# A decoder step on one core: sample tokens' attention scores moved to TensorE, weight splits moved to VectorE, one value stripe moved behind the second turn

## The reference, cut to what matters

```python
def mem_kv(mem, g, w_kv):                       # 256 memory tokens, once
    kv = rmsnorm(mem, g) @ w_kv                 # 1024 x 2048 weights
    k, v = jnp.split(kv, 2, axis=-1)
    return (k.reshape(B, M, X_HEADS, X_HEAD_DIM), v.reshape(B, M, X_HEADS, X_HEAD_DIM))

def cross_attend(h, mk, mv, w_q, w_o):          # 4 heads of 256, M = 256
    q = (h @ w_q).reshape(B, L, X_HEADS, X_HEAD_DIM)
    s = jnp.einsum('blhd,bmhd->bhlm', q, mk) * (X_HEAD_DIM ** -0.5)
    p = jax.nn.softmax(s, axis=-1)
    o = jnp.einsum('bhlm,bmhd->blhd', p, mv)
    return o.reshape(B, L, D_MODEL) @ w_o
```

## Time and profile before

| | us |
|---|---|
| median of 3 runs (1449.26 to 1451.04) | 1449.39 |
| the profiled execution | 1445.97 |
| its span, first to last instruction | 1444.1 |
| PE busy in the span | 1409.5 |
| PEld (weight loads) busy | 1368.8 |
| DVE busy | 893.8 |
| POOL busy | 631.0 |
| ACT busy | 421.6 |

### The profile page before, as it was taken

How to read it: one execution, slowest core, us unless ns; L and a number is a source line. 1 busy time by engine, 2 the same in 40 slices (tenths; PEclk the granted TensorE clock), 3 DMA queues, 4 the chain that set the end, 5 groups by cost and what they waited for, 6 DMA issues and landing times.

```text
span 1444.1 us, 25449 instructions
## 1 busy us (share of the span) xinstructions
PE 1409.5 (98%) x9871; PEld 1368.8 (95%) x9871; DVE 893.8 (62%) x1465; ACT 421.6 (29%) x635; POOL 631.0 (44%) x479
## 2 busy tenths in 40 slices
PE   8999999999999996999999999999999999999997
PEld 7999999989999975889999999999999999999996
DVE  4325677778752268647997666766676658632335
ACT  6131344470020144520042222222223223311111
POOL 1241246045531166314572877787778710000163
PEclk9999999999999999999999999999999999999999
DMA  9412111102161266321123222122222142423113
GB/s 293 125 44 81 51 30 38 37 23 59 44 190 45 87 241 197 117 88 44 44 59 88 89 84 77 59 87 87 73 68 77 59 133 95 168 89 110 36 44 117
DMA packets 163567, 129.18 MB, mean 89 GB/s; under 512 B 11532, under 2 KB 148748, under 8 KB 163363
## 3 DMA queue, kind: packets, MB, share of 16 engines
q1 hardware_dynamic: 163499, 128.25, 28.6%
HBM read 107.88 MB, written 20.58 MB: 89 GB/s over the span
## 4 chain that ended last, share of the span: by engine, by line
PE 71%; POOL 10%; issue 9%; DVE 5%; ACT 2%; DMA 2%; SPq 1%; POOLq 0%; DVEq 0%; ACTq 0%
PE pm L2294 18%; PE pm L2296 18%; PE pm L2295 18%; PE pm L2565 3%; PE pm L2567 3%; PE pm L2566 3%; POOL gb L1040 2%; POOL raw L1022 2%; POOL raw_c L1022 2%; POOL sum L1029 1%; POOL sum L1027 1%; DMA xt<-in_x_prompt 1%; DVE acc L2210 1%; PE pm L2427 1%; POOL raw_c L1034 1%
## 5 line engine op out<-in xcount | busy, mean ns | idle before, releaser
L2294 PE MATMUL pm<-x_hi,w_hi 128*128 128x344 f32 x960 | 310.6, 323 | 0.3 <-DVE gb L1654 0.3
L2296 PE MATMUL pm<-x_hi,w_lo 128*128 128x344 f32 x960 | 306.6, 319 | 0.0
L2295 PE MATMUL pm<-x_lo,w_hi 128*128 128x344 f32 x960 | 306.6, 319 | 0.0
L1126 ACT ACTIVATE w_hi<-raw 128x1024 fp32r<-128x1024 f32 x88 | 93.3, 1060 | 531.7 <-PE pm L2296 455.1
L2294 PEld LDWEIGHTS pm<-x_hi,w_hi 128*128 128x128 f32 x960 | 180.4, 188 | 2.1 <-issue 1.5
L2295 PEld LDWEIGHTS pm<-x_lo,w_hi 128*128 128x128 f32 x960 | 180.4, 188 | 0.2
L2296 PEld LDWEIGHTS pm<-x_hi,w_lo 128*128 128x128 f32 x960 | 180.4, 188 | 0.0
L843 POOL TENSOR_TENSOR raw<-raw,gains 128x1024 f32<-128x1024 f32 x32 | 63.6, 1992 | 128.2 <-DMA raw<-in_w_in 81.3
L1587 DVE TENSOR_TENSOR w_lo<-raw,w_hi 128x1024 fp32r<-128x1024 f32 x79 | 112.9, 1429 | 10.5 <-ACT w_hi L1126 10.4
L925 POOL TENSOR_TENSOR fp<-acc 128x344 f32 (+1 forms) x22 | 21.3, 967 | 201.8 <-DVE acc L2252 196.9
L2141 DVE TENSOR_TENSOR gb<-gb,ga 128x1032 f32<-128x1032 f32 x19 | 53.0, 2788 | 89.9 <-POOL gb L1040 89.9
(11 more groups left out here) (376 smaller groups left out, 4052.6 us busy)
## 6 DMA issues: line engine op xcount, KB each, us to landing
raw<-in_w_ffn_in SPq DMA_DIRECT2D x24, 512.0 KB, 4.2
sg_raw<-s_rows SPq DMA_DIRECT2D x22, 516.0 KB, 5.1
s_rows<-gb SPq DMA_DIRECT2D x21, 516.0 KB, 2.7
raw<-in_w_in SPq DMA_DIRECT2D x20, 512.0 KB, 3.8
raw_c<-in_w_ffn_in SPq DMA_DIRECT2D x20, 512.0 KB, 5.0
raw<-in_w_out SPq DMA_DIRECT2D x8, 512.0 KB, 3.7
raw<-in_w_cq SPq DMA_DIRECT2D x8, 512.0 KB, 3.5
ke<-in_cache_mem_k SPq DMA_DIRECT2D x8, 512.0 KB, 6.7
```

Of the source, the lines that this page charges most:

```text
L1126: act.activation(w_hi[s][:, :, :], src, ACT.Copy).then_inc(hi_made, 1)
L2294: pe.matmul(out, w_hi[s][:, k, :], hi[:, k, x0:x0 + cols], start=(k == 0), stop=False)
L2295: pe.matmul(out, w_hi[s][:, k, :], lo[:, k, x0:x0 + cols], start=False, stop=False)
L2296: last = pe.matmul(out, w_lo[s][:, k, :], hi[:, k, x0:x0 + cols], start=False, stop=(k == kb - 1))
```

## The change

- Cached keys come in by features, rearranged on the host (`cache_k_cols`), 1 MB for a sample in two loads into `sk[b % 2]`; `load_keys` waits until PE has used that buffer (`sk_done`).
- Scores of sample b are 8 matmuls on PE (`sample_scores`): the weights are 8 columns of `qsp` (the samples' queries, zero but for sample b's column, scaled by -SCALE), the moving side is 256 cached tokens; head h writes partitions 32h to 32h+7 of bank 7. All samples add up in that bank, which DVE zeroes first. They stand after the key stripes 1, 3, 5, 7 and between value stripes. The spreading (`sample_q`), the turn of the queries ahead of it and the DVE dot products are gone.
- DVE makes the low halves of all kv stripes from 1 on and of the first two stripes of `co` (`split_low`). POOL makes `query_rest` of all eight blocks.
- The scale -SCALE goes into the keys' halves, so `maxima` is one reduction (ALU.min) and no product behind it.
- The last value stripe moves from before `scores_(1)`'s turn to behind `turn_p(1)`; the second half of the values (`value_round(1, ...)`, `value_kept(1, ...)`) follows it. `raw_b` moves to another place, so its loads wait for `mem_sq`. The samples' values are computed for samples 3 and 4 in block 5 and for 5 in block 6 (before: 3 in block 5, 4 and 5 in block 6).

The core of the diff:

```diff
@@ load_keys (SP) @@
                     if b >= 2:
-                        sp.wait_ge(ssc_made, 2 * b + s - 2)
-                    sp.dma_start(keys[b % 2][s][:, :],
-                                 k_rows[b * M + s * P:b * M + (s + 1) * P, :]).then_inc(kc_in[b % 2][s], 16)
+                        sp.wait_ge(sk_done, b)
+                    sp.dma_start(sk[b % 2][:, 4 * s:4 * s + 4, :], t["cache_k_cols"][b, :, 4 * s:4 * s + 4, :]
+                                 ).then_inc(kc_in[b % 2][s], 16)
...
@@ sample_values (POOL) @@
+                for n in range(2):
+                    query_rest(n)
                 value_rest(0)
-                pool.wait_ge(evac, p.done)
+                for n in range(2, 4):
+                    query_rest(n)
+                pool.wait_ge(sk_done, NS + 1)
...
-                query_rest(3)
-                split_behind(ph["co"], 0, 0)
                 value_rest(1)
                 query_rest(4)
...
@@ keys_values (ACT) @@
+                for i in range(7):
                     if i == 6:
                         value_round(0, 0)
                         value_round(0, 1)
+                    split_next(p, i, 0, False)
+                    if i < 2:
+                        q_block(i)
+                    if i in (3, 4):
+                        key_round(i - 3)
+                    split_next(p, i, 1, False)
                 q_block(2)
                 exps(0)
+                split_next(p, 7, 0, False)
+                q_block(3)
+                exps(1)
+                sample_softmax()
+                turned_round(0)
                 split_next(p, 7, 1, True)
...
@@ keys_values, maxima (DVE) @@
+            def split_low(m):
+                n = (p, m // 2, m % 2) if m < 16 else (ph["co"], 0, m - 16)
+                count = n[0].first + 2 * n[1] + n[2]
+                dve.wait_ge(lo_made, count)
+                dve.wait_ge(hi_made, count + 1)
+                dve.tensor_tensor(w_lo[n[2]][:, :, :], raw_slot(*n)[0], w_hi[n[2]][:, :, :].bitcast(F32),
+                                  ALU.subtract).then_inc(lo_made, 1)
...
             def maxima(n):
                 dve.wait_ge(sc_done, n + 1)
-                dve.tensor_reduce(smax[:, :], wide(0).rearrange("p (h m) -> p h m", h=H), AX_X,
-                                  ALU.max).then_inc(mx_step, 1)
-                dve.wait_ge(mx_step, n + 1)
-                dve.tensor_scalar(nmax[:, :], smax[:, :], -SCALE, None, ALU.mult).then_inc(mx_made, 1)
+                dve.tensor_reduce(nmax[:, :], wide(0).rearrange("p (h m) -> p h m", h=H), AX_X,
+                                  ALU.min).then_inc(mx_made, 1)
...
+                split_low(1)
+                for j in range(KB):
+                    turned_evac(j)
+                    split_low(j + 2)
+                split_low(10)
                 key_rest(0)
+                split_low(11)
                 key_rest(1)
-                sample_scores(5, 0)
+                split_low(12)
                 value_kept(0, 0)
                 value_kept(0, 1)
-                sample_scores(5, 1)
+                split_low(13)
+                split_low(14)
                 maxima(0)
...
                 normalize(0)
-                sample_scores(7, 1)
+                split_low(15)
                 maxima(1)
-                value_kept(1, 0)
-                value_kept(1, 1)
+                sample_maxima()
                 normalize(1)
+                sample_normalize()
                 turned_rest(0)
+                split_low(16)
...
@@ attention (DVE) @@
                     turned_rest(n)
+                    if n == 1:
+                        value_kept(1, 0)
+                        value_kept(1, 1)
+                        split_low(17)
...
@@ keys_values (PE) @@
+                def sample_scores(b):
+                    for s in range(2):
+                        pe.wait_ge(kc_in[b % 2][s], K_BASE + 16 * (b // 2 + 1))
...
                     for d in range(2):
+                        for h in range(H):
+                            last = pe.matmul(bank[7][32 * h:32 * h + NS, 0:M], qsp[:, b, 2 * h + d, :], sk[b % 2][:, 2 * h + d, :],
+                                             start=(b == 0 and d == 0), stop=(b == NS - 1 and d == 1))
+                    last.then_inc(sk_done, 1)
...
+                    sample_scores(i)
+                for n in range(7):
                     value_stripe(n)
+                    if n in (1, 3):
+                        sample_scores(4 + n // 2)
+                    if n == 4:
+                        scores_(0)
                     if n == 5:
-                        scores_(0)
-                        sample_q(7)
-                    if n == 6:
+                        sample_scores(6)
                         scores_(1)
                         turn_p(0)
+                        sample_scores(7)
...
@@ attention (PE) @@
                     turn_p(n)
                     if n == 1:
-                        turn_scores()
-                    if n == 2:
                         turn_weights()
-                    for b in ((), (), (), (0,), (1, 2), (3,), (4, 5), (7,))[n]:
+                        value_stripe(7)
+                    for b in ((), (), (), (0,), (1, 2), (3, 4), (5,), (7,))[n]:
```

More of the change, by code:

```diff
@@ L729, in _ @@
                     sp.wait_ge(sq_added, 8 * NC)
+                    sp.wait_ge(mem_sq, 2)
                     for i in (1, 2):
@@ L935, in final_squares @@
                     one(LAST, s, c, 6 * LAST + q, q % 2)
[L937 to L962, removed]
             def query_rest(n):
@@ L1365, in keys_values @@
                 act.wait_ge(evac, ph["kv"].done)
-                for a in range(0, P, 32):
-                    last = act.activation(qdup[:, :, a:a + NS], qT[:, :, TP:T], ACT.Copy)
-                last.then_inc(qd_made, 1)
[L1370 to L1378, removed]
-                        key_round(1)
-                        q_block(1)
+                for b0, b1 in ((0, NS - 1), (NS - 1, NS)):
+                    at = keep[:, 65 * b0:65 * b1] if b0 == 0 else keep[:, 65 * b0:512]
+                    spots = (at.rearrange("p (b r) -> p b r", b=NS - 1) if b0 == 0 else at.unsqueeze(1))[:, :, 0:57:8]
+                    last = act.activation(spots, qT[:, :, TP + b0:TP + b1].rearrange("p k b -> p b k"), ACT.Copy,
+                                          scale=-SCALE)
+                last.then_inc(qd_made, 1)
+                for i in range(7):
                     if i == 6:
@@ L1980, in key_rest @@
                     dve.wait_ge(k_round, KR + n + 1)
-                    dve.tensor_tensor(k_lo[:, 4 * n:4 * n + 4, :], kT[:, 4 * n:4 * n + 4, :],
-                                      k_hi[:, 4 * n:4 * n + 4, :].bitcast(F32), ALU.subtract).then_inc(k_rest, 1)
-                def value_kept(c, a):
-                    dve.wait_ge(v_round, VR + 2 * c + a + 1)
-                    if (c, a) == (0, 0):
-                        dve.wait_ge(mem_sq, 4)
-                        dve.wait_ge(lo_made, p.first + 14)
-                    dve.tensor_scalar(vnat[:, a, c * 512:(c + 1) * 512], bank[4 * c + a][:, :], rtok[:, 9 + a:10 + a], None,
-                                      ALU.mult).then_inc(evac, 2)
@@ L2657, in keys_values @@
                         stripe_chunk(p, i, s, 0, m_hi, m_lo, cols=M, out=bank[4 + s][:, 0:M])
-                        if i == 0 and s == 0:
-                            pe.wait_ge(qd_made, 1)
-                            for k in range(KB):
-                                last = pe.matmul(wide(2)[:, k * P:(k + 1) * P], qdup[:, k, :], ident[:, :],
-                                                 start=True, stop=True)
-                            last.then_inc(qn_turned, 1)
-                        if i and s == 0:
-                            sample_q(i)
@@ L2674, in keys_values, with value_stripe @@
                     if n == 5:
-                        scores_(0)
-                        sample_q(7)
-                    if n == 6:
+                        sample_scores(6)
                         scores_(1)
                         turn_p(0)
+                        sample_scores(7)
+            def value_stripe(n):
+                p = ph["kv"]
+                c, q, s = n // 4, n % 4, n % 2
+                pe.wait_ge(lo_made, p.first + KB + n + 1)
+                if n == 4:
+                    pe.wait_ge(evac, p.done + KB)
+                for a in range(2):
+                    for k in range(2):
+                        mh, ml = (m[:, 2 * q + k, a * P:(a + 1) * P] for m in (m_hi, m_lo))
+                        wh, wl = (w[s][:, 4 * k:4 * k + 4, :].rearrange("p a c -> p (a c)") for w in (w_hi, w_lo))
+                        pe.matmul(bank[4 * c + a][:, :], mh, wh, start=(q == 0 and k == 0), stop=False)
+                        pe.matmul(bank[4 * c + a][:, :], ml, wh, start=False, stop=False)
```

(4 more changed lines are left out.)

204 lines of the change are left out of this document (65 added, 139 removed).

## The result

The changed kernel takes **1440.56 us** (median of 5 runs, 1439.51 to 1441.32), the kernel before 1449.39: ratio 0.9939, 95% interval 0.9925 to 0.9952, 8.8 us less. The forecast was 1437.4, in a range of 1431.0 to 1446.0. The profiled execution took 1440.80.

What follows compares the result with a forecast made beforehand. PE was taken as the bound, with the attention's start hanging on VectorE. Gains of 2.1 (keys) and 10.4 (values to block 4) less 0.6 (rest) made 11.9 us, from 1449.39 to 1437.4; range 1431 to 1446.

Steps and rivals of the forecast that it cites:

- A: The keys' stretch on PE, from 30.0 us to 27.9, a gain of 2.1.
- B's work: PE's work from the values to block 4's scores, without waits: 45.0 us.
- B: Stretch from the values to block 4's scores: from 59.7 us to 49.3, a gain of 10.4.
- Block 3's does not: Block 3's softmax is not covered by PE's work: exps(3) ends 12.3 us after the turn, PE's work 10.4; wait 2.0.
- Part C: Stretch from block 4's scores to co: from 47.5 us, a loss of 0.6.
- the wait at stripe 11: PE waits 1.4 us at value stripe 11, behind the keys' low half, which waits for kT's store, 6.4 us to land.
- The wait at block 2: PE waits 0.4 us at scores_(2), as POOL passes hold VectorE between normalize(0) and maxima(1).
- Rival 2: VectorE is late more often and the clock falls: gain 6.8 us, time 1442.6; chance 0.20.
- Sample 6's wait: Samples 3 and 4 come one block earlier, so sample 6's values are there in time and its 2.45 us wait goes.
- The 2.6 at the first sample: PE waits 2.6 us at the first sample's values, as its probabilities stand on POOL behind value_rest(1) and query_rest(4).
- Sample 7's 0.4: Sample 7's load still starts behind sample 5, so it is late: 0.4 us more.
- Rival 5: VectorE still bounds the attention's start, w_lo passes replacing dot products; the values' stretch keeps its 59.7 us: 1447.9; chance 0.07.

Runs made afterwards that it cites:

- e4_all: Changed kernel with three queue orders: block 4's queries first on POOL, stripe 11's low half before the keys', maxima before stripes 15 to 17's low halves; 1426.62 us.
- e1_q4: Changed kernel with block 4's query low half ahead of the low half of the values' second half on POOL; 1435.48 us.
- e3_max: Changed kernel with the maxima of blocks 1 to 3 ahead of the weights' low halves of stripes 15 to 17 on VectorE; 1437.76 us.
- before_again: Kernel before, unchanged, profiled a second time; one execution, 1447.94 us.
- changed_again: Changed kernel run once more as it is, on another chip; 1439.5 us, ratio 0.9939 to the kernel before.
- e2_low11: Changed kernel with stripe 11's weights' low half ahead of the keys' low half on VectorE; 1435.59 us.
- e7_dots: e4_all with low halves of stripes 1 to 14 on POOL, query blocks 0 and 1's on VectorE, plus 64 unread VectorE passes; 1431.30 us.
- e9_three: e7_dots with value stripe 7 in front again and the maxima in two steps again, with the tiny product; 1438.72 us.
- e5_v7: e4_all with value stripe 7 in front again, right behind stripe 6, as in the kernel before; 1430.96 us.
- e4_again: The same kernel as e4_all, on another chip; 1426.86 us, ratio 0.9851 to the kernel before.
- e8_twice: e4_all with every sample's score product done twice into the same sums; 1432.60 us.

## Why the prediction was right or wrong

- **Direction and range: right, the number in part by luck.** Forecast 1437.4 (1449.39 less 11.9 is 1437.5; the rounding slipped), measured 1440.56, inside 1431 to 1446. But the profiled pair, on which the sum was made, gained 5.2 of the 11.9 (1445.97 to 1440.80). The median comes nearer to the forecast because the kernel before has slower executions than the profiled one, which the forecast did not account for: 3.7 of the 8.8.
- **A: right.** 28.36 against 27.9. A sample's product is 0.98 (forecast 1.0); the wait at stripe 1 is 0.52 (0.7); a stripe is 2.97 and not 2.9, 0.6 over eight.
- **B's work: right.** 45.0 forecast, 45.3 after, 45.06 with its last waits in e4_all.
- **The step that failed** is in Part B: "Block 3's does not ... so `exps(3)` ends about 12.3 after the turn ... Wait 2.0." That line followed VectorE and ACT alone. `exps(3)` was done at 576.58, 11.3 after the turn (the passes that the line names add up to 12.8, not 12.3) and 1.1 behind PE, so this part was even too pessimistic; but the scores of block 4 need a second thing, `query_rest(4)`, and that stands on POOL behind `value_rest(1)`. PE waited 6.08 for it where the forecast had 2.0. The forecast knew this queue: Part C walks it, for the samples' probabilities, "behind `value_rest(1)` and `query_rest(4)`", and prices 2.6 there. It asked who waits for the end of the queue and not who waits for each pass in it. e1_q4 shows that this was it.
- **Mis-sized in B:** the wait at stripe 11 was 2.47 (1.4), as the store took 7.7 to land and not 6.4; with 6.5, in e1_q4, it was 1.33. The wait at block 2 was 1.47 (0.4): `w_lo` of stripe 15 stood ahead of `maxima(1)` and took 3.39 beside two POOL passes in a row, a meeting longer than the one taken from the earlier trace rows. e3_max, with that order turned round, has no wait there.
- **Rival 2 came in part.** The clock fell twice, for 1.6 and 1.8 us, behind waits of 2.47 and 6.08. The forecast itself had counted no fall.
- **C: right in its work and in one term of three.** Without the 1.8 of lower clock it is 44.9, e4_all's 44.88. Sample 6's wait is gone as forecast. The 2.6 at the first sample never showed, since block 4's scores had waited longer for the same queue; in e1_q4 and e4_all it did not show either: there `value_rest(1)` is followed by the probabilities at once. Sample 7's 0.4 did not come.
- **Rival 5 came near in B, but not for its reason.** B kept 57.1 of its 59.7. Yet e4_all has the same passes on VectorE in another order, and a B of 45.06: it was the order in the queues and not VectorE's load.
- **What the gain hung on: too narrow.** The forecast put B's 10.4 in the main on the dot products and `nmax`. In e4_all's order the moved stripe is worth 4.2, the low halves 2.7, and the dot products' time, undone on top of the low halves, 1.8. What the parts are worth in the change as it came, without these orders, no run shows.

## What to carry to other kernels

When passes move to another engine's queue, list for each pass in that queue its first reader and the time it is needed; a pass that waits for a DMA belongs behind every pass that TensorE needs and that doesn't wait for it. Then look at the same queue for work that only has to be done some day (here the low halves of stripes 15 to 17) and put it behind what the next product reads. A wait of some 2 us or more can also cost what the clock loses behind it (1.6 and 1.8 us in this case): price both.

## What the runs showed of the hardware

- **The clock behind a wait.** The profiled executions, between 495 and 640 us, show this. Behind waits of PE of 3.6 to 6.2 us the granted clock was at 0.50 (1.2 GHz) each time, seven of seven (3.64 and 4.09 in before_again, 4.09 in before, 6.08 in after, 6.21 in changed_again, 6.04 in e2_low11, 5.84 in e3_max); behind the last four the scores of 2.85 us took 4.5 to 5.3. Behind waits of 1.8 to 2.9 it fell to 0.50 in seven (1.81 in e7_dots, 2.08 in e9_three, 2.28 in e5_v7, 2.40 in before and in before_again, 2.47 in after, 2.92 in changed_again) and not in four (2.45 in before, 2.48 in e9_three, 2.58 in e3_max, 2.66 in e1_q4). What tells these apart is open; the length of the wait alone does not. Each kind in one kernel, e3_max by stretch, behind 2.58 and behind 5.84:

```profile
536.40:539.50 3.10, 3.05 (x16) 2.24 (x20) 2.82 (x3) 0.69 (x1) 0.00 (x0) 1.00 0.61 130
576.90:582.30 5.40, 5.33 (x25) 5.33 (x26) 0.00 (x0) 0.00 (x0) 2.90 (x4) 0.50 0.00 0
```

- **A store that lands late or not.** kT's store of 1024 KB took 7.7 us after, 8.1 in changed_again, 7.7 to 7.8 in e2_low11, e3_max and e4_all, 8.1 in e4_again, and 6.5 in e1_q4, issued within 0.5 us of the same moment in all seven. From after to e1_q4, 1.2 us less of landing made 1.1 us less of PE's wait.
- **Four heads side by side.** 16 records of 8 columns of weights and 256 moving columns took 0.98 us, and a repeat took 0.86 more (e8_twice).
